# Two mixers' head reordered: full products ahead of the convolution's transposes, states interleaved, one split moved to VectorE

## The reference

```
z, xbc, dt_raw, cq, ckv, kr, gates = split_cols(u @ w_in[l], IN_SPLIT_SIZES)
xbc = jax.nn.silu(causal_depthwise_conv(xbc, conv_w, conv_b))     # 4 taps, 3072 channels
xs, bm, cm = split_cols(xbc, (SSD_D_INNER, SSD_GROUPS * SSD_STATE, SSD_GROUPS * SSD_STATE))
dt = jax.nn.softplus(dt_raw.astype(jnp.float32) + dt_bias.astype(jnp.float32))
y = ssd_chunked_scan(xh, dt, a, bm, cm) + xh.astype(jnp.float32) * d_skip...[:, None]
y = rms_norm(y * jax.nn.silu(z), norm_g)
```

## Time and profile before

| | |
|---|---|
| time, median of 3 runs | 2731.54 us (2731.43 to 2731.8) |
| the profiled execution | 2731.43 us, span 2729.6 us |
| PE busy | 2697.4 us, 99% of the span |
| DVE busy | 1470.8 us, 54% |
| ACT busy | 1343.6 us, 49% |
| POOL busy | 701.0 us, 26% |
| granted clock of TensorE | 1.00 |
| DMA | 461.23 MB, mean 169 GB/s |

### The profile page before, as it was taken

One profiled execution on the slowest core, in us unless ns is written; L12 is line 12 of the kernel. 1 busy time (PEld: TensorE's weight loads), 2 busy tenths in 40 slices (PEclk: granted clock), 3 DMA queues, 4 the chain that ended last, 5 costly groups with the idle time before them and its releaser, 6 DMA issues.

```text
span 2729.6 us, 32283 instructions
## 1 busy us (share of the span) xinstructions
PE 2697.4 (99%) x12892; PEld 2217.4 (81%) x12892; DVE 1470.8 (54%) x2238; ACT 1343.6 (49%) x1560; POOL 701.0 (26%) x161
## 2 busy tenths in 40 slices
PE   8999999999999999999999999999999999999999
PEld 7887778888888778888888887788888887877887
DVE  4438873333448763433457885543334488865333
ACT  5335664334345654343357574443443475745432
POOL 3440014444420024444413000044443211000443
PEclk9999999999999999999999999999999999999999
DMA  7554445556554445555554244355555553443553
GB/s 240 186 176 166 162 141 186 185 172 202 187 183 154 154 140 191 187 180 201 185 185 160 79 157 155 135 185 185 185 190 185 171 172 98 154 160 117 190 187 131
DMA packets 209928, 461.23 MB, mean 169 GB/s; under 512 B 9458, under 2 KB 31604, under 8 KB 209780
## 3 DMA queue, kind: packets, MB, share of 16 engines
q1 hardware_dynamic: 209236, 458.12, 49.5%
q10 hardware_dynamic: 544, 1.05, 0.1%
HBM read 458.09 MB, written 1.05 MB: 168 GB/s over the span
## 4 chain that ended last, share of the span: by engine, by line
PE 89%; DVE 5%; ACT 3%; issue 2%; POOL 1%; DMA 0%; SPq 0%; DVEq 0%; ACTq 0%
PE banks L323 27%; PE banks L325 27%; PE banks L324 27%; PE banks L417 3%; ACT w_hi L286 2%; PE banks L672 2%; DVE w_lo L262 1%; PE banks L1458 1%; PE banks L1472 1%; PE banks L695 1%; POOL w_lo L262 1%; PE banks L684 0%; DVE h_lo L465 0%; ACT h_hi L447 0%; PE banks L886 0%
## 5 line engine op out<-in xcount | busy, mean ns | idle before, releaser
L286 ACT ACTIVATE w_hi<-raw 128x2048 fp32r<-128x2048 f32 (+1 forms) x441 | 833.2, 1890 | 1139.1 <-PE banks L325 1090.9
L262 POOL TENSOR_TENSOR w_lo<-raw,w_hi 128x2048 fp32r<-128x2048 f32 (+1 forms) x149 | 686.8, 4611 | 1647.6 <-ACT w_hi L286 1647.6
L262 DVE TENSOR_TENSOR w_lo<-raw,w_hi 128x2048 fp32r<-128x2048 f32 (+2 forms) x292 | 674.1, 2312 | 603.3 <-ACT w_hi L286 597.1
L323 PE MATMUL banks<-w_hi,h_lo 128*128 128x512 f32 x2336 | 920.6, 394 | 5.9 <-DVE w_lo L262 2.6
L325 PE MATMUL banks<-w_hi,h_hi 128*128 128x512 f32 x2336 | 905.1, 387 | 0.0
L324 PE MATMUL banks<-w_lo,h_hi 128*128 128x512 f32 x2336 | 904.1, 387 | 0.0
L323 PEld LDWEIGHTS banks<-w_hi,h_lo 128*128 128x128 f32 x2336 | 438.7, 188 | 108.7 <-issue 16.3
L325 PEld LDWEIGHTS banks<-w_hi,h_hi 128*128 128x128 f32 x2336 | 438.7, 188 | 90.7
L324 PEld LDWEIGHTS banks<-w_lo,h_hi 128*128 128x128 f32 x2336 | 439.2, 188 | 83.8
L323 PE MATMUL banks<-w_hi,act_lo 128*128 128x512 f32 x704 | 276.1, 392 | 0.9 <-POOL w_lo L262 0.9
L325 PE MATMUL banks<-w_hi,act_hi 128*128 128x512 f32 x704 | 274.2, 389 | 0.0
(11 more groups left out here) (273 smaller groups left out, 2521.9 us busy)
## 6 DMA issues: line engine op xcount, KB each, us to landing
raw<-in_ffn_w SPq DMA_DIRECT2D x124, 1024.0 KB, 5.0
raw<-in_w_in SPq DMA_DIRECT2D x108, 1024.0 KB, 5.0
raw<-in_ffn_w_down SPq DMA_DIRECT2D x44, 1024.0 KB, 4.8
raw<-in_ffn_w_gate SPq DMA_DIRECT2D x40, 1024.0 KB, 5.0
raw<-in_ffn_w_up SPq DMA_DIRECT2D x40, 1024.0 KB, 5.0
raw<-in_w_ssd_out SPq DMA_DIRECT2D x16, 1024.0 KB, 4.9
raw<-in_w_branch SPq DMA_DIRECT2D x8, 1024.0 KB, 4.8
raw<-in_w_out SPq DMA_DIRECT2D x8, 1024.0 KB, 4.8
```

The costliest lines, as they stand in the source:

```text
L262: eng.tensor_tensor(w_lo[:, c % SPLIT, 0:kc * n], raw[:, c % RAW, 0:kc * n], w_hi[:, c % SPLIT, 0:kc * n].bitcast(F32), ALU.subtract).then ...
L286: self.eng.activation(w_hi[:, c % SPLIT, 0:kc * n], raw[:, c % RAW, 0:kc * n], ACT.Copy).then_inc(hi_made, 1)
L323: pe.matmul(ps, al, bh, start=first, stop=False)
```

## The change

On TensorE, `turn_xbc(p - 1)` moves from the middle of `xb{p}` to its end; the maps, `turn_xbc(3)` and `turn_x(0)` follow `xb4`; `turn_xbc(4)` and `turn_x(1)` follow `xb5`; `turn_x(2)` comes after the first chunk of `z0`, and the `cT` turns and `turn_x(3)` after its third quarter. The states go one by one, each with the former one's `of` behind it, where they had gone in pairs. ScalarE copies `xb{p}` ahead of the taps of group p - 1, and silu 2 and 3 come in other places. VectorE has `lo(12)` ahead of the maps and `lo(15)` for `lo(14)`, `x_groups` 1 and 2 one place earlier, `kr` and two weighings ahead of the low parts of `cT`, `kr` by a copy for a maximum with itself, and weighing 2 and 3 each ahead of a state's read. The low part of chunk 15 is made by VectorE, where GpSimd made it.

```
             for p in range(6):
-                xb = product(pe, banks, chunks, f"xb{p}", h, KD)
-                if p == 4:
-                    maps_of_states()
-                if p:
-                    next(xb)
+                finish(product(pe, banks, chunks, f"xb{p}", h, KD))
+                if p and p != 4:
                     turn_xbc(p - 1)
-                    if p == 5:
-                        turn_x(0)
-                finish(xb)
...
+                if p == 4:
+
+                    pe.wait_ge(*banks.of(convolved, 2))
...
+                    turn_xbc(3)
+                    turn_x(0)
+            turn_x(1)
             m1 = product(pe, banks, chunks, "m1", h, KD)
...
             next(z_steps[0])
-            turn_x(1)
+            next(z_steps[0])
+            turn_x(2)
             next(z_steps[0])
...
-            next(z_steps[0])
-            turn_x(2)
             turn_x(3)
             finish(z_steps[0])
-            for g in range(0, GROUPS, 2):
-                state_of(g)
-                state_of(g + 1)
-                off_of(g)
-                off_of(g + 1)
+            for g in range(GROUPS + 1):
+                if g < GROUPS:
+                    state_of(g)
+                if g:
+                    off_of(g - 1)
...
             for p in range(6):
                 if p >= 2:
                     spa.was_filled(f"xbT{p - 2}.1")
-                if p:
-                    taps(p - 1)
-                if p >= 2:
-                    silu(p - 2)
+                if p == 5:
+                    silu(3)
+                for i in range(TT):
+                    ps, read = spa.read(f"xb{p}.{i}")
+                    copied(act, xbc_tok[:, p % 2, i, :], ps, i, read)
+                if p == 4:
+                    silu(2)
                 if p == 4:
                     ps, read = spa.read("Bt")
                     act.activation(B_tok[:, :], ps, ACT.Copy).then_inc(read[0], 1)
-                for i in range(TT):
-                    ps, read = spa.read(f"xb{p}.{i}")
-                    copied(act, xbc_tok[:, p % 2, i, :], ps, i, read)
+                if p:
+                    taps(p - 1)
+                if p in (2, 3):
+                    silu(p - 2)
...
             convolve(2)
+            lo(12)
             for j in range(TT):
                 ps, read = spv.read(f"cb{j}")
...
-            lo(12)
             convolve(3)
-            lo(14)
+            lo(15)
             x_groups(0)
             convolve(4)
+            x_groups(1)
             convolve(5)
-            x_groups(1)
-            for q in range(3):
-                low_turned(spv, f"cT{q}", c_hi, c_lo, 2 * q, lora_g)
+            x_groups(2)
             for i in range(TT):
                 spv.was_read(f"m1.{i}")
-            v.link(dve.tensor_tensor(kr[:, :, :], tail[:, :, 800:864], tail[:, :, 800:864], ALU.max))
+            v.link(dve.tensor_copy(kr[:, :, :], tail[:, :, 800:864]))
...
             weigh(0)
             weigh(1)
-            x_groups(2)
+            for q in range(3):
+                low_turned(spv, f"cT{q}", c_hi, c_lo, 2 * q, lora_g)
             x_groups(3)
             for g in range(GROUPS):
-                if g == 0:
-                    spv.before("st0")
-                    weigh(2)
-                    weigh(3)
+                if g + 2 < GROUPS:
+                    spv.before(f"st{g}")
+                    weigh(g + 2)
...
-            return ["GV"[c not in (1, 15, 16, 17, 18, 19)] for c in range(len(chunks))]
+            return ["GV"[c not in (1, 16, 17, 18, 19)] for c in range(len(chunks))]
```

More of the change, by code:

```diff
@@ L1381, in turn_x @@
                     mm.then_inc(done, 1)
[L1383 to L1395, removed]
-            for p in range(6):
-                xb = product(pe, banks, chunks, f"xb{p}", h, KD)
-                if p == 4:
-                    maps_of_states()
-                if p:
-                    next(xb)
+            for p in range(6):
+                finish(product(pe, banks, chunks, f"xb{p}", h, KD))
+                if p and p != 4:
                     turn_xbc(p - 1)
-                    if p == 5:
-                        turn_x(0)
-                finish(xb)
                 if p == 2:
@@ L1413, in mix2_pe @@
                     pe.matmul(ps[:, 64:96], ones[:, :], dta[:, 0, :], start=True, stop=True).then_inc(done, 1)
+                if p == 4:
+                    pe.wait_ge(*banks.of(convolved, 2))
+                    for j in range(TT):
+                        ps, done = banks.begin(pe, f"cb{j}", "a")
+                        for g in range(GROUPS):
+                            tok = slice(j * P, (j + 1) * P)
+                            mm = pe.matmul(ps[:, g * P:(g + 1) * P], xbcT[:, 16 + g, tok], xbcT[:, 20 + g, tok],
+                                           start=True, stop=True)
+                        mm.then_inc(done, 1)
+                    ps, done = banks.begin(pe, "Bt", "a")
+                    for g in range(GROUPS):
+                        mm = pe.transpose(ps[:, g * P:(g + 1) * P], xbcT[:, 16 + g, 0:P], ident)
+                    mm.then_inc(done, 1)
+                    turn_xbc(3)
+                    turn_x(0)
+            turn_x(1)
             m1 = product(pe, banks, chunks, "m1", h, KD)
```

## The result

The changed kernel takes 2753.31 us (median of 4 runs, 2752.92 to 2754.59), the kernel before 2731.6 us. The ratio is 1.0081, with a 95% interval of 1.0062 to 1.0098: slower by 21.7 us. The forecast was 2749 us in a range of 2740 to 2755.

A forecast was written before the change was run, and what follows sets the result against it. TensorE, whose matmuls fill all but 32 us of the span, was taken as the bound. Waits of 1.7 + 4.1 + 3.8 less 0.7 give 8.9 us a layer, 17.8 for two, on 2731.5: 2749 us, range 2740 to 2755.

The forecast's parts named there:

- Breaks up to `xb5`: Break behind `xb4`: `turn_x(0)` waits for silu 2 and the copy of `Bt`, so `xb5` starts 1.7 us late.
- T4: The end of the product `xb4` on TensorE, from which the forecast counts times.
- `turn_x(1)` and `turn_xbc(5)`: Breaks behind `xb5` and in `m1`: waits for `x_groups(0)`'s reads and convolution 4's end, 4.1 us a layer together.
- T5: The end of the product `xb5` on TensorE, from which the forecast counts times.
- `turn_x(3)`: Break in `z0`: its second bank waits for `cT0`'s low part, behind `kr` and weighings held by GpSimd; 3.8 us a layer.
- the bound: Lower bound of the wait in `turn_x(3)`: 0.6 us if GpSimd held neither `kr` nor the weighing behind it.
- States: From the end of `z0` to the start of `R1`: 10.4 us instead of 11.1, a gain of 0.7 us a layer.
- rival 3: TensorE's clock falls to 1.2 GHz in the waits: 5.6 us more for both layers, 2755 us; chance 0.04.
- rival 2: More is late: chunk 10's low part delays `xb4` by up to 2.3 us a layer, 2754 us; chance 0.12.
- rival 1: In `z0` VectorE comes ahead of GpSimd and is not held: 3.2 us a layer less, 2743 us; chance 0.10.
- rival 5: No change: waits of about 9 us a layer are taken back later by TensorE, 2732 us; chance 0.03.
- rival 4: Faster: states' new order alone counts, earlier breaks' waits being satisfied in time; 2.8 us less, 2729 us; chance 0.05.

The follow-up runs named there:

- experiment 4: Changed kernel with `turn_x(0)` between the two chunks of `xb5` instead of ahead of them: 2752.97 us, with one run at 2750.19.
- Experiment 3: Changed kernel with `turn_xbc(5)` behind both chunks of `m1` instead of between them: 2752.69 us.
- experiment 2: Changed kernel with the low parts of `cT` ahead of `kr` and the two weighings on VectorE, as before the change: 2745.38 us.
- 8: Changed kernel with the edits of experiment 2, Experiment 3 and experiment 4 together: 2741.84 us.
- 5: Changed kernel with chunk 19's low part made by VectorE instead of GpSimd: 2744.65 us.
- 6: Changed kernel with `kr` made by a maximum of `tail` with itself instead of a copy, at its new place: 2753.37 us.
- 10: Changed kernel with the low parts of `cT` ahead of `kr` and the weighings, and the states in pairs again: 2742.33 us.
- experiment 1: Changed kernel with TensorE kept busy by repeated transposes in its two longest waits, in `turn_xbc(5)` and `turn_x(3)`: 2748.74 us.
- experiment 11: Kernel before the change with `x_groups(2)` ahead of `kr` and the first two weighings, low parts of `cT` staying first: 2728.8 us against 2731.6.
- 9: Changed kernel with the states in pairs again and weighings 2 and 3 both ahead of them: 2752.66 us.

## Why the prediction was right, point by point

- **Breaks up to `xb5`, 1.7 us.** Right: T4 + 5.5 measured. TensorE waited 0.65 us for the reading of `cb0` and 0.52 us for silu 2. I had booked all of it to the silu, whose chain does decide when `turn_x(0)` opens (T4 + 4.6, forecast 4.7). But I called the reading of `cb0` at T4 + 3.4 covered, and it is itself waited for; so taking the silu's wait away leaves the other (4). Each wait also costs the 0.16 us by which rows overlap otherwise.
- **`turn_x(1)` and `turn_xbc(5)`, 4.1 us together.** Right: 10.6 us from T5 to `m1`'s second chunk, where 10.5 was worked out. But these are not waits that one could have back one by one, as the sum with its separate terms reads. Experiment 3 took one away and gained next to nothing: convolution 5 came no sooner, and what VectorE won behind it was lost in the weighings that GpSimd held. Only together with experiment 2's order did such moves gain (8).
- **`turn_x(3)`, 3.8 us.** Right: 3.5 and 3.8 us measured in the two layers, taken away by another order (2), by another maker of chunk 19 (5), and not by another form of `kr` (6). Experiment 3's rows show the sentence on which the bound rested, that the weighing would be held if `kr` were not. The Trainium skill ("SBUF — State Buffer", under "SBUF: two separate sides") has whichever engine starts first hold the shared pair of ports for a whole instruction. The traces agree: 3.61 us for the copy and 5.63 for the two weighings against 0.23 and 1.29, the copy ending 0.1 us after GpSimd's instruction and the weighings 1.15 us after it.
- **States, 0.7 us gained.** Right for the stretch (10.4 us worked out and measured, 11.1 before), wrong as a price of this part. One by one costs 0.7 to 0.8 us a layer; the stretch is shorter because `x_groups(2)` now stands ahead of `kr`, worth 1.4 (the table in 10). It isn't the long wait in `turn_x(3)` that gave VectorE the time: in 2 and 10 that wait is 0.6 us, and the stretch is no longer.
- **Clock.** This is the term that the sum put at nothing. I gave rival 3 a chance of 0.04 as an alternative; it came on top of the forecast, and chunks at a lower clock, which the prediction names as a sign of being wrong, are there. Four stretches behind waits took 4.9 us longer than at full speed (10.82 and 4.34 against 9.38 and 2.83, 10.35 and 3.82 in the fourth layer), where the rival's price was 5.6 us; experiment 1 gives back 4.6 us. This is the difference between 2749 and 2753.3 us. With it the time lies outside the forecast's own 2746 to 2752; it lies inside 2740 to 2755 because that range was drawn to take in rivals 2 and 3, so this much of being right is luck. My evidence against was the earlier trace rows, idle time at the start with the clock at 1.00. It didn't carry over to the middle of the kernel: from 1505 to 1512 us TensorE was busy for 3.45 us of 7, and then the clock fell. The Trainium skill ("TensorE: Matmul & The Clock Gate", Part 1) has the clock fall after idle time, and the runs agree with that: with the two waits filled there is no fall (1).
- **The other rivals.** GpSimd came 1.0 us ahead of `kr` (1504.92 against 1505.94), where the forecast had a margin of 1.1. The two did meet in the other order in experiment 3, and it gained nothing, since the weighing was held in `kr`'s place: rival 1's price was wrong, whatever its chance. The low part of chunk 10 (rival 2) was in time: no wait of TensorE for a low part of weights stands in the head. Nothing was absorbed later (rival 5), and rival 4's gain came by another way, in experiment 11.

The sum of the waits was 17.8 us; with the clock held up, the kernel is 17.1 to 17.4 us slower. The 21.7 us split by the order in which the parts are put in: the head's new order alone costs 10.7 us (10), the states one by one on top of it 3.0 (2 against 10), and `kr` and the weighings ahead of the low parts 7.9 (the changed kernel against 2). Each figure has its share of the clock in it; of the 3.0 us the stretch accounts for 1.4.

What stays open is why the clock falls behind the same wait in one place and not in the next, and so what of experiment 4's shift is real. In the profiled runs it fell at every wait of 3.5 us or more in `turn_x(3)` (ten of ten, in the changed kernel and in 3, 4, 6 and 9), at the wait of 2.4 us in `turn_xbc(5)` eight times of twelve (the changed kernel, 2, 5, 6, 9, 10), and at its 1.9 us in experiment 4 not at all (two).

## What to carry to other kernels

When TensorE is busy 99% of the time, moving its breaks to tidier places is paid by whatever chain those breaks started: count from the break to the last reader of its bank, and compare that with the work TensorE has until it needs the bank again. Removing one such wait helps only if nothing further down the same chain holds it; look first at which engine is the late one. And where GpSimd has long instructions, put VectorE's operations with an input in PSUM in their time, and those with two inputs in SBUF, or copies within SBUF, behind them: that is what made experiment 11 the fastest version.

## What the runs showed of the hardware

- A copy of 128 x 128 between places in SBUF on VectorE took 0.23 us beside an idle GpSimd and 3.61 us beside a busy one; a maximum of a tile with itself 0.29 and 3.68 us; two products of 128 x 512 from two tiles in SBUF 1.29 and 5.63 us. `x_groups`, with one input in PSUM, kept its 0.68 to 0.69 us an instruction beside a busy GpSimd (11).
- TensorE's clock fell to its lower level behind waits of 2.4 us (eight times of twelve) and of 3.5 to 3.8 us (eight of eight). Matmuls of 512 columns then followed each other at 0.43 us instead of 0.23. Transposes that write the waiting bank again and again kept it at 1.00, and TensorE's other waits stayed as they were to 0.1 us.
- With the clock falling, the changed kernel's four runs spread over 1.7 us; with it held up, the four of experiment 1 over 0.6 us. Four runs don't make that more than a hint: experiment 2's four spread over 0.6 us too, and the clock fell twice in its profiled run.
